# Attention of a two-layer encoder step: masked logit rows are kept in SBUF and turned by TensorE, in place of logits made a second time transposed; the layer loop is written out

## The reference, cut to what matters

```python
score = jnp.where(adm[None], score, -jnp.inf)
_, idx = lax.top_k(score, topk)
valid = key_chunk[idx] <= q_chunk[None, :, None]
logits = jnp.einsum('bqhgd,bqkhd->bqhgk', q, kg) * (HEAD_DIM ** -0.5)
logits = jnp.where(valid[:, :, None, None, :], logits, -jnp.inf)
p = jax.nn.softmax(logits, axis=-1)
o = jnp.einsum('bqhgk,bqkhd->bqhgd', p, vg)
```

## Time and profile before

| | |
|---|---|
| time, median of 3 runs | 3827.07 us (3825.92 to 3831.55) |
| span of the profiled execution | 3823.0 us |
| the median less that span | 4.1 us |
| busy in the span | PE 92%, DVE 51%, ACT 16%, POOL 31% |
| attention stage, first layer | 605.10 to 871.85 us |
| attention stage, second layer | 2506.4 to 2773.15 us |

### The profile page before, as it was taken

One profiled execution on the slowest core, in us unless ns is written; L12 is line 12 of the kernel. 1 busy time (PEld: TensorE's weight loads), 2 busy tenths in 40 slices (PEclk: granted clock), 3 DMA queues, 4 the chain that ended last, 5 costly groups with the idle time before them and its releaser, 6 DMA issues.

```text
span 3823.0 us, 51426 instructions
## 1 busy us (share of the span) xinstructions
PE 3512.2 (92%) x19968; PEld 3242.8 (85%) x20004; DVE 1957.8 (51%) x2743; ACT 621.5 (16%) x829; POOL 1186.9 (31%) x497
## 2 busy tenths in 40 slices
PE   3989997999969999999749899979999699999996
PEld 2989995559969999999739899945599699999996
DVE  4249996644255151414372599965451642424244
ACT  2330111221121010101123201112201210101010
POOL 6013331003433343434350233300034343434341
PEclk8989997999969999999869899979999699999998
DMA  4111222003121111112121112220031211111121
GB/s 160 46 56 48 81 91 77 19 1 125 44 109 44 44 44 44 44 44 90 41 87 55 51 45 85 89 73 17 1 131 44 109 44 44 44 44 44 44 90 57
DMA packets 75377, 234.16 MB, mean 61 GB/s; under 512 B 12816, under 2 KB 25456, under 8 KB 73712
## 3 DMA queue, kind: packets, MB, share of 16 engines
q1 hardware_dynamic: 33552, 122.57, 10.4%
q10 hardware_dynamic: 41696, 109.88, 7.8%
HBM read 176.37 MB, written 56.05 MB: 61 GB/s over the span
## 4 chain that ended last, share of the span: by engine, by line
PE 71%; DVE 20%; issue 5%; ACT 2%; POOL 1%; ACTq 1%; DVEq 0%; POOLq 0%
PE PS L401 50%; DVE PASS L1252 10%; PE PS L467 5%; PE PS L615 4%; PE PS L581 3%; PE PS L497 2%; PE PS L604 1%; PE PS L600 1%; DVE X L1061 1%; PE PS L583 1%; PE PS L601 1%; PE PS L602 1%; DVE TC L1272 1%; PE PS L481 1%; DVE RANK L1306 1%
## 5 line engine op out<-in xcount | busy, mean ns | idle before, releaser
L401 PE MATMUL PS<-H,W 128*128 128x358 f32 x9792 | 1646.0, 330 | 63.5 <-ACT H L994 34.6
L401 PEld LDWEIGHTS PS<-H,W 128*128 128x128 f32 x9792 | 1636.1, 192 | 70.5 <-ACT H L994 39.8
L337 POOL TENSOR_TENSOR W<-RAW,ones 128x1024 fp32r<-128x1024 f32 x216 | 420.3, 1946 | 2438.0 <-PE PS L401 2063.1
L401 PE MATMUL PS<-A,W 128*128 128x358 f32 x5760 | 950.0, 327 | 0.0
L401 PEld LDWEIGHTS PS<-A,W 128*128 128x128 f32 x5760 | 948.3, 189 | 1.5 <-issue 1.5
L339 POOL TENSOR_TENSOR W<-RAW,W 128x1024 fp32r<-128x1024 f32 x216 | 610.5, 2827 | 17.0
L1252 DVE TENSOR_SCALAR_CACHE_REDUCE PASS<-SC,TC,CST 48x176 bf16<-48x176 f32 x496 | 408.7, 882 | 2.6 <-DVE TC L1267 0.4
L1437 DVE TENSOR_TENSOR X<-X,PS 128x1074 f32 (+1 forms) x64 | 81.5, 1274 | 593.2 <-PE PS L401 593.2
L467 PE MATMUL PS<-WQ,H 128*128 128x364 f32 (+1 forms) x1296 | 237.4, 339 | 52.0 <-DVE H L1072 37.1
L467 PEld LDWEIGHTS PS<-WQ,H 128*128 128x128 f32 (+1 forms) x1296 | 211.1, 184 | 67.4 <-issue 41.2
L1425 DVE TENSOR_TENSOR SQ<-SQ,RS 128x1074 f32<-128x1074 f32 x64 | 117.1, 1830 | 260.3 <-ACT SQ L1007 259.8
(11 more groups left out here) (129 smaller groups left out, 2402.2 us busy)
## 6 DMA issues: line engine op xcount, KB each, us to landing
RAW<-in_w_slab SPq DMA_DIRECT2D x216, 512.0 KB, 3.6
x_keep<-X ACTq DMA_DIRECT2D x32, 537.0 KB, 2.7
gates<-GS ACTq DMA_DIRECT2D x32, 537.0 KB, 2.9
XT<-x_keep ACTq DMA_DIRECT2D x8, 2148.0 KB, 12.0
RAW<-in_w_qkv SPq DMA_DIRECT2D x16, 546.0 KB, 3.6
GA<-gates ACTq DMA_DIRECT2D x16, 537.0 KB, 3.7
GB<-gates ACTq DMA_DIRECT2D x16, 537.0 KB, 4.6
qs_keep<-QH ACTq DMA_DIRECT2D x16, 512.0 KB, 2.6
```

Source lines behind the costliest of these rows:

```text
L337: g_.tensor_tensor(hi, raw, one, ALU.mult).then_inc(hi_split, 1)
L401: mm = nc.tensor.matmul(PS[:, b0 + c, 0:CW], W[:, s, w, k, :], act[:, a, k, c * CW:(c + 1) * CW], start=(first and w == 0 and a == 0), sto ...
```

## The change

Each head's logits are made once, by query row. Two buffers of PSUM take them in turn (banks 0 and 1, 2 and 3); a row block of 1040 keys is split into the 1024 prompt keys and a unit of its own that holds the 16 meta keys of the four heads. VectorE adds the mask, scales by minus an eighth, writes the row block to SBUF (PA, PB; three groups deep) and takes the row's least value in one tensor_tensor_reduce. ScalarE takes the exponential in place, with that least value as its bias and the row's sum as a second output. VectorE inverts the sum, one column, and scales the row block in place. TensorE then turns the blocks of a step, one head at a time, by `transpose` with a float32 identity into banks 4 and 5; ScalarE copies them to PT; the product with V stays as it was, and VectorE copies O out of PSUM without a division. Row logits run two groups ahead of the steps and exponentials one. The mask holds 0 and -1e30, for which each of the 8 ranked tiles gets one more operation at the end of the top-k part. The loops over the layers of all engines are written out.

```diff
@@ -92,6 +92,18 @@
     return [(N_META + P * j, P * j, P, j) for j in range(t + 1)] + [(0, META0, N_META, SPECIAL)]
+def row_pieces(t):
+    return pieces(t) if EXT[t] <= 1024 else [(0, 0, 512), (512, 512, 512)]
+NGRP = 9 * NKV
+ROW_UNITS = [(i, g) for i in range(NGRP) for g in range(0 if EXT[ORDER[i // NKV]] <= 1024 else -1, GROUP)]
+ROW_NO = {u: k for k, u in enumerate(ROW_UNITS)}
+NROW = len(ROW_UNITS)
...
+        PA = at("PA", [P, 2 * GROUP, LONG], F32, r_k + 12288)
+        PB = at("PB", [P, GROUP, LONG], F32, r_x)
+        O2 = at("O2", [P, 2, 2, P], F32, r_k + 12288 + 2 * GROUP * LONG * 4)
+        def prob(i, g):
+            return PA[:, i % 3 * GROUP + g, :] if i % 3 < 2 else PB[:, g, :]
...
-            with pe.Fori(0, DEPTH) as l:
+            for l in range(DEPTH):
...
-                def logits(a, h):
+                def logits(i, g):
+                    a, kv = divmod(i, NKV)
                     t = ORDER[a]
-                    m, kv = ROWS[t], h // GROUP
-                    if h == 0 and a < 2:
-                        pe.wait_ge(ks_in[a], (l + 1) * 16)
-                    if h == 0:
+                    m, k = ROWS[t], ROW_NO[i, g]
+                    if kv == 0 and (i, g - 1) not in ROW_NO:
+                        if a < 2:
+                            pe.wait_ge(ks_in[a], (l + 1) * 16)
                         pe.wait_ge(qs_in[a % 3], (l * 3 + a // 3 + 1) * 16)
-                    if narrow(a):
-                        if h_no(a, h) > 2:
-                            pe.wait_ge(max_done, l * 72 + h_no(a, h) - 2)
+                    if k >= 2:
+                        before, q = ROW_UNITS[k - 2]
+                        if q < 0:
+                            pe.wait_ge(tail_masked, (l * NKV + before % NKV + 1) * GROUP)
+                        else:
+                            pe.wait_ge(masked, (l * NGRP + before) * GROUP + q + 1)
+                    c0 = 1024 * (k % 2)
+                    if g < 0:
+                        units = [(q, N_META * q, META0, N_META) for q in range(GROUP)]
                     else:
-                        pe.wait_ge(max_done, l * 72 + h_no(a, h))
-                    c0 = logit_col(a, h)
-                    for dst, key, w in pieces(t):
-                        out = flat[0:m, c0 + dst:c0 + dst + w]
+                        units = [(g, dst, key, w) for dst, key, w in row_pieces(t)]
+                    for q, dst, key, w in units:
                         for x in range(2):
-                            nc.tensor.matmul(out, QS[:, a % 3, h, 0:m], KS[:, 2 * kv + x, key:key + w],
-                                             start=(x == 0), stop=False)
-                        last = nc.tensor.matmul(out, bigI[0:m, 0, 0:m],
-                                                MB[0:m, MB_OFF[t] + dst:MB_OFF[t] + dst + w],
-                                                start=False, stop=True)
+                            last = nc.tensor.matmul(flat[0:m, c0 + dst:c0 + dst + w],
+                                                    QS[:, a % 3, GROUP * kv + q, 0:m],
+                                                    KS[:, 2 * kv + x, key:key + w],
+                                                    start=(x == 0), stop=(x == 1))
                     last.then_inc(logit_done, 1)
-                def logits_t(u):
+                def turn_p(u):
                     a, kv, kt = STEPS[u]
-                    t = ORDER[a]
+                    t, i = ORDER[a], NKV * a + kv
                     m = ROWS[t]
-                    dst, key, w, _ = key_tiles(t)[kt]
...
+                    dst, _, w, _ = key_tiles(t)[kt]
+                    if u >= 2:
+                        pe.wait_ge(pt_made, l * NU + u - 1)
+                    for g in range(GROUP):
+                        if kt == 0:
+                            pe.wait_ge(p_ready, (l * NGRP + i) * GROUP + g + 1)
+                        last = nc.tensor.transpose(PS[0:w, 4 + u % 2, g * m:(g + 1) * m],
+                                                   prob(i, g)[0:m, dst:dst + w], cst["ident"][0:m, 0:m])
+                    last.then_inc(turned_p, 1)
...
-                for h in range(NH):
-                    logits(0, h)
-                logits_t(0)
-                logits_t(1)
+                for i, g in ROW_UNITS:
+                    if i < 2:
+                        logits(i, g)
+                turn_p(0)
                 for u, (a, kv, kt) in enumerate(STEPS):
-                    if u + 2 < NU:
-                        logits_t(u + 2)
+                    i, n = NKV * a + kv, len(key_tiles(ORDER[a]))
+                    for j, g in ROW_UNITS:
+                        if j == i + 2 and min(max(g, 0), n - 1) == kt:
+                            logits(j, g)
+                    if u + 1 < NU:
+                        turn_p(u + 1)
                     values(u)
-                    for h in range(GROUP):
-                        if a + 1 < 9 and h * len(key_tiles(ORDER[a])) // GROUP == kt:
-                            logits(a + 1, GROUP * kv + h)
...
+                def exponent(i, g):
+                    t, c = ORDER[i // NKV], i % 3 * GROUP + g
+                    m, row = ROWS[t], prob(i, g)[0:ROWS[t], 0:EXT[t]]
+                    act.wait_ge(masked, (l * NGRP + i) * GROUP + g + 1)
+                    nc.scalar.activation(row, row, ACT.Exp, bias=LEAST[0:m, c:c + 1], scale=-1.0,
+                                         accum_out=DEN[0:m, c:c + 1]).then_inc(exp_done, 1)
+                for g in range(GROUP):
+                    exponent(0, g)
                 i = 0
                 for u, (a, kv, kt) in enumerate(STEPS):
-                    t = ORDER[a]
-                    m, w = ROWS[t], key_tiles(t)[kt][2]
-                    act.wait_ge(lt_done, l * NU + u + 1)
+                    t, now = ORDER[a], NKV * a + kv
+                    m, w, n = ROWS[t], key_tiles(t)[kt][2], len(key_tiles(t))
+                    if kv == 0 and kt == 0 and 0 < a < 7:
+                        q_load(a + 2)
+                    act.wait_ge(turned_p, l * NU + u + 1)
                     if u >= 3:
                         act.wait_ge(pv_done, l * NU + u - 2)
-                    nc.scalar.activation(PT[0:w, u % 3, 0:GROUP * m], PS[0:w, 3 + u % 3, 0:GROUP * m],
-                                         ACT.Exp, scale=HD ** -0.5).then_inc(pt_made, 1)
-                    if u in ENDS and kv == 0 and a > 0 and a + 2 < 9:
-                        q_load(a + 2)
+                    copy(PT[0:w, u % 3, 0:GROUP * m], PS[0:w, 4 + u % 2, 0:GROUP * m]).then_inc(pt_made, 1)
+                    for g in range(GROUP):
+                        if now + 1 < NGRP and min(g, n - 1) == kt:
+                            exponent(now + 1, g)
...
+                    did(V_.tensor_scalar(mask, mask, BIG, None, ALU.mult))
+                    settled()
...
-                def maximum(a, h):
...
+                def mask_row(i, g):
+                    a = i // NKV
+                    t, k = ORDER[a], ROW_NO[i, g]
+                    m, c0, c = ROWS[t], 1024 * (k % 2), i % 3 * GROUP + g
+                    dve.wait_ge(logit_done, l * NROW + k + 1)
+                    if i >= 3:
+                        dve.wait_ge(turned_p, l * NU + ENDS[i - 3])
+                    if g < 0:
+                        for q in range(GROUP):
+                            last = V_.tensor_tensor_reduce(
+                                prob(i, q)[0:m, 0:N_META], flat[0:m, c0 + N_META * q:c0 + N_META * (q + 1)],
+                                MB[0:m, MB_OFF[t]:MB_OFF[t] + N_META], -HD ** -0.5, 3e38, ALU.add, ALU.min,
+                                TAIL[0:m, q:q + 1])
+                            last.then_inc(tail_masked, 1)
+                        return
+                    first, w = row_pieces(t)[0][1], sum(w for _, _, w in row_pieces(t))
+                    lo, start = EXT[t] - w, 3e38
+                    if lo:
+                        dve.wait_ge(tail_masked, (l * NKV + i % NKV) * GROUP + g + 1)
+                        start = TAIL[0:m, g:g + 1]
+                    V_.tensor_tensor_reduce(prob(i, g)[0:m, lo:lo + w], flat[0:m, c0:c0 + w],
+                                            MB[0:m, MB_OFF[t] + lo:MB_OFF[t] + lo + w], -HD ** -0.5, start,
+                                            ALU.add, ALU.min, LEAST[0:m, c:c + 1]).then_inc(masked, 1)
+                def normalise(i, g):
+                    t, c, n = ORDER[i // NKV], i % 3 * GROUP + g, (l * NGRP + i) * GROUP + g + 1
+                    m, row_ = ROWS[t], prob(i, g)[0:ROWS[t], 0:EXT[t]]
+                    dve.wait_ge(exp_done, n)
+                    V_.reciprocal(RDEN[0:m, c:c + 1], DEN[0:m, c:c + 1]).then_inc(rden_made, 1)
+                    dve.wait_ge(rden_made, n)
+                    V_.tensor_scalar(row_, row_, RDEN[0:m, c:c + 1], None, ALU.mult).then_inc(p_ready, 1)
                 def outputs(i):
                     a, kv = divmod(i, NKV)
```

(26 more changed lines are left out.)

94 lines of the change are left out of this document (20 added, 74 removed).

## The result

The changed kernel takes 3700.2 us (median of 4 runs, 3699.1 to 3704.5) against 3826.5 for the kernel before (4 runs beside it, 3825.4 to 3831.6): a ratio of 0.9672, 95% interval 0.9659 to 0.9686, 126 us less. The forecast was 3710, in 3680 to 3778.

A forecast was written before the change was run, and what follows sets the result against it. TensorE's work was taken to bound the attention stage: 173 work, 19 waits and 13 slow clock make 205 us against 267. 3823.0 - 124 + 6.4 = 3705 of span, plus 4.1: 3710 us, range 3680 to 3778.

The forecast's parts named there:

- The stage is bound by TensorE, work removed is time gained: Attention stage: a microsecond of TensorE work removed is one gained; 267 to 205 us, 62 per layer, 124 in all.
- The turn, the term on which all hung: Turning blocks of P on TensorE: 0.11 us per turn taken, between 0.105 and 0.38; 38 us a layer.
- rival B: Each turn takes two passes of 0.105 us: stage 231 us, time 3761; chance 0.15.
- Row logits: TensorE's logits by query row lose the mask product and some overhead: 51 us a layer, 77 before.
- VectorE: Attention stage: VectorE work of 132 us against 140 before, staying under TensorE's.
- Rival D: Masked rows run at half rate, so VectorE becomes the bound: stage 245 us, time 3790; chance 0.08.
- Waits: TensorE idle in the attention stage: 15 us in six short groups plus 4 at the start; bounds 10 to 35.
- PE work: TensorE work in the attention stage after the change: 173 us a layer against 239.
- The clock: Low clock at the stage's start after idling: 13 us lost, as before; above 0.95 from some 40 us on.
- Mask scalings: Eight added scalings before the stage, 0.2 to 0.6 us each: 3.2 us a layer, 6.4 for both, range 1.4 to 8.
- The loop at 0: Layer loop written out: twice the code may cost or save -4 to +5 us, taken as 0.
- End of the stage at no gain: Stage end: 3.37 us of reciprocals go, but the first half slab of the merge already covers them, so no gain.

The follow-up runs named there:

- e3: Changed kernel with each turn as a plain float32 product with the identity in place of the transpose; 3799.7 us, ratio 0.9923.
- e4: Changed kernel with each turn as a float32r product with a rounded identity, row blocks held as float32r; 3731.1 us, ratio 0.9746.
- e7: Changed kernel plus unread identity products that keep TensorE at work while it waits for the last mask operations; 3714.8 us, ratio 0.9703.
- e8: Changed kernel with mask scalings folded into existing operations and 66 identity products during TensorE's wait for masks; 3699.7 us, ratio 0.9664.
- e11: Changed kernel with folded mask scalings and identity products both during the mask wait and in the short groups' gaps; 3694.2 us, ratio 0.9645.
- e10: Changed kernel with identity products both during the mask wait and in the short groups' gaps, mask scalings kept; 3699.0 us, ratio 0.9668.
- e1: Kernel before the change with only each engine's layer loop written out; 3832.3 us, ratio 1.0011.
- e2: Changed kernel without the eight mask scalings, their factor folded into existing operations; 3702.2 us, ratio 0.9668.

## Why the prediction was right

The mechanism was the one forecast, and the sum missed by 10 us, or 8% of the gain. Inside the stage its terms were off in opposite directions (waits too long, work and clock too short), so the closeness of 205 is in part luck.

- **The stage is bound by TensorE, work removed is time gained.** Right: 127.1 us from the two stages, 124 forecast.
- **The turn, the term on which all hung.** Taken as 0.11 between 0.105 and 0.38, measured 0.11. e3 gives the price of the other choice, 0.22 and 95 us in the stages. That is rival B's two passes, which I had priced at 51: I counted 30 a layer for 72 steps with four absorbed, and e3 shows 46 to 49. The 16 narrow steps were left out, whose turns also have 128 columns each: 88 x 4 x 0.11 = 39. The waits absorbed 3, and the rest was not traced. B would have been 3800, not 3761. The mean of one turn in the groups is 280 ns, but four end within 0.44: what one takes by itself is not what it costs in a stream. The Trainium skill (TensorE: Matmul & The Clock Gate, Part 4: PE-mode transpose) gives about 275 ns, which agrees with that mean and not with the spacing. On its second statement, that transposes don't count as busy for the clock: the mean granted clock is 0.948 with transposes and 0.936 with the products of e4, so no run here bears it out.
- **Row logits.** A unit of 912 keys is 0.93 us where the terms gave 0.76 + 0.23 = 0.99: near.
- **VectorE.** 132 forecast, 112.7 measured, but the terms were right. The durations of its records add up to 127.8: masked rows 60 (60 forecast), reciprocals and scalings 48 (50), copies of O 13 (15), low parts 6 (7). Busy time is less because records overlap: an accumulator read lies within the pass before it, and the next operation starts under that pass's end. The step that failed is adding up single durations as if nothing overlapped. A row of 1024 takes 1.28. Rival D, half rate, is excluded by that row. ACT: 112 forecast, 111.0 measured.
- **Waits.** 19 a layer forecast, some 9 idle us measured, 8.1 of it before turns. The chain of copy, exponential and scaling is a few tenths late per head, not 2.5 a group. So TensorE is 95% busy in the stage, where the sign to look for was 85%.
- **PE work.** 173 forecast. Busy 192 and 196 us, less the lost clock of 14 and 18, is 178 in both stages: 5 over, not traced to one term.
- **The clock.** 13 a layer forecast, on the ground that it would be as before. By the stretches above the first stage runs 20 us at 0.50, 20 at 0.96 and 20 at 0.83, which is 10 + 0.8 + 3.4 = 14 us of lost clock (the second loses 18); not all of it is on the path (e7 won 0.5 by its first 4 us at full clock). The size was near, the cause given for it was wrong: e7 removed the idle time, and the clock fell all the same. Also wrong was that it would be above 0.95 from some 40 us on: that came at 60. So the waits were 10 too many, the work 5 too few and the clock 1 to 5 too few, and 173 + 19 + 13 = 205 met 201 and 205.
- **Mask scalings.** 3.2 a layer forecast, 4.0 measured from the end of the search to the first row logit. Half of the scalings' own 4.5 us is one row beside POOL's split, which the sum had not in it; but the split fell on the scan before. Seven of the eight are in the 0.2 to 0.6 named, that one is not. Without them 3.6 come back in the first layer and 2.1 in the second (e8 against e7, e11 against e10).
- **The loop at 0.** Nothing was gained, as forecast; e1 has +4, a ratio whose interval begins at 1.0001.
- **End of the stage at no gain.** Right; the parts of O are made under the first merge slab.
- **The 10 us between 3710 and 3700.** Of span it is 3705 to 3697.3: 3 more from the stages, 5 less beside them (6.4 forecast, 1.4 measured). The other 1.2 is the median's distance from the span, 2.9 where I had added 4.1. Each run has its own span on record, and its time stands 1.8 us above it for the changed kernel and some 2.2 for the one before; the rest of both distances is that the profiled execution was not the median one.

What stays open is why the clock falls in the first 8 us of the stage and by which course it comes back. The runs exclude two things as the sole cause of the fall: the long idle time before the stage, and the gaps before turns. Two rivals are untested. The short idle pieces around the first row logits were never filled, and all of these starts have the special tile's groups with their narrow operands in common; a kernel with another tile first was not tried.

## What to carry to other kernels

A turn of a float32 tile through TensorE costs 0.11 us per 128 x 128 block in a stream if it is written as a transpose, and 0.22 as a plain float32 product: look for one instruction or two in the rows before you cost one. Where products recompute transposed what exists already in rows, price the turn plus the copy that the old form needed anyway. Before a few us are credited to an edit, look at the granted clock of each stretch and at operations that share time with POOL: here these moved single layers by 4 to 14 us whatever the edit. The worth of folding the masks, 5.7 us, could not be read from e2's median; it came from two pairs of profiles, part by part. And before a busy time is forecast from single rows, look whether such rows overlap: VectorE's 128 us of records filled 113.

## What the runs showed of the hardware that was not expected

- The granted clock takes different courses after the low start of a stage, in the same kernel and with the same instructions. By ten us from the twentieth on, e7 has 0.94, 1.00, 0.83, 0.83, 1.00 in one layer and 0.67, 0.67, 0.84, 0.84, 0.83, 0.66, 0.69 in the other, stages of 200.8 and 214.4 us. There are more than two: the changed kernel's second stage has 0.87, 0.66, 0.83, 0.84, 0.99, and e2's 0.67, 0.67, 0.84, 0.84, 0.92.
- The clock fell to 0.50 some 4 us into the stage after 20 us at 1.00 with TensorE 90% busy (e7). In e10 it fell after 4 us at 1.00 without a pause and stayed at 0.50 for 13.4 us of unbroken work.
- A bf16 scaling of 784 columns took 2.38 us beside POOL's splitting of a slab, one of 1040 took 0.43 alone: a factor of more than five. POOL's operations of that split take 1.9 and 2.95 us here. The Trainium skill (SBUF — State Buffer, SBUF: two separate sides) tells of a port pair that VectorE and GpSimd take in turn as an exclusive lock; the rows agree with a wait for POOL's operation, since the scaling starts at 591.53, within POOL's, and ends at 593.91, 0.2 us behind it.
